# A hybrid decoder layer on eight cores: the unused output of a squaring moved to another tile, decode staging in two buffers, the decode projection in eight pieces, smaller first tables

## The reference, cut to what matters

```
def layer_inputs(h, norm_w, w_in, pos):
    hn = rms_norm(h, norm_w)
    proj = hn @ w_in
    ...
    u, gp, q, k, v, gr = jnp.split(proj, [o1, o2, o3, o4, o5], axis=-1)
    q = rotary(split_heads(q).astype(jnp.float32), pos)
    k = rotary(split_heads(k).astype(jnp.float32), pos) * (HEAD_DIM ** -0.5)
...
    # prompt group: fresh sequences, zero initial state
    u, gp, q, k, v, gr = layer_inputs(h_p, norm_w[l], w_in[l], pos_p)
    pool_o, buf_p = pool_mixer(u, buf0, pos_p, w_pool[l], pool_scale[l])
    S_p, ret_o = retention_prompt(q, k, v, log_g)
    h_p = h_p + merge_branches(pool_o, gp, ret_o, gr, ret_norm_w[l], w_out[l])
    # sample group: continue from carried state
    ...
```

## Time and profile before

| what | value |
|---|---|
| median of 3 runs (lowest to highest) | 598.63 us (596.15 to 598.93) |
| the profiled execution's own time | 599.85 us |
| span of its slowest core (core 6); all cores | 598.3 us; 589.3 to 598.3 us |
| PE / PE weight load busy | 561.6 us (94%) / 317.7 us (53%) |
| DVE / ACT / POOL busy | 389.7 / 264.7 / 110.4 us |
| DMA | 79.05 MB, 132 GB/s over the span |

### The profile page before, as it was taken

The page is one execution under the profiler, slowest core; times in us unless marked ns, Lnnn a source line. Parts: engine busy times, 40 slices in busy tenths (PEclk is TensorE's granted clock), DMA queues, the critical chain, the costliest instruction groups (busy, mean ns, idle before and its releaser), DMA issues.

```text
span 598.3 us, 13978 instructions; the slowest of 8 cores (589.3 to 598.3 us)
## 1 busy us (share of the span) xinstructions
PE 561.6 (94%) x4540; PEld 317.7 (53%) x4540; DVE 389.7 (65%) x1010; ACT 264.7 (44%) x822; POOL 110.4 (18%) x133
## 2 busy tenths in 40 slices
PE   2799998988999998999999999999999999999994
PEld 1244455674545544565564646546464646556672
DVE  3358645657865856668557676868577683954665
ACT  3245454743532632543434545454453544544332
POOL 4330001120200112111112222140322220221010
PEclk9799998997999999999999999999999999999898
DMA  8999996597444624523356764567664662627203
GB/s 166 208 172 211 168 189 146 104 119 138 89 98 103 147 89 109 160 76 90 107 143 163 160 154 134 130 191 142 181 126 138 139 161 95 143 91 153 41 3 110
DMA packets 76066, 79.05 MB, mean 132 GB/s; under 512 B 55566, under 2 KB 58270, under 8 KB 74060
## 3 DMA queue, kind: packets, MB, share of 16 engines
q1 hardware_dynamic: 71836, 56.63, 37.7%
q0 software_dynamic: 4016, 21.28, 20.7%
q10 hardware_dynamic: 144, 0.26, 0.1%
HBM read 64.86 MB, written 18.41 MB: 139 GB/s over the span
## 4 chain that ended last, share of the span: by engine, by line
PE 83%; DMA 7%; DVE 4%; issue 3%; ACT 2%; POOL 1%; SPq 0%; DVEq 0%; POOLq 0%; ACTq 0%
PE pp L592 44%; PE pp L904 18%; PE pp L609 8%; DMA w_in_bf<-w_in 2%; PE pp L845 2%; DMA pbp<-F 2%; PE pp L826 2%; DMA hnTs<-hn 2%; PE pp L967 2%; PE pp L714 1%; PE pp L755 1%; PE pp L757 1%; PE pp L731 1%; PE pp L546 1%; DMA xr<-x 1%
## 5 line engine op out<-in xcount | busy, mean ns | idle before, releaser
L592 PE MATMUL pp<-w_in_bf,hnTs 128*128 128x512 bf16 x1120 | 261.6, 385 | 1.9 <-DMA w_in_bf<-w_in 1.1
L592 PEld LDWEIGHTS pp<-w_in_bf,hnTs 128*128 128x128 bf16 x1120 | 106.0, 99 | 124.0 <-issue 14.3
L904 PE MATMUL pp<-w_out_bf,yT 128*128 128x512 bf16 (+1 forms) x464 | 100.5, 372 | 0.8 <-PE pp L904 0.2
L511 POOL TENSOR_TENSOR sm<-sm,nh 128x4 f32<-128x4 f32 (+2 forms) x49 | 44.5, 908 | 262.1 <-DVE sm L508 258.2
L630 ACT ACTIVATE F<-pp,pack 128x128 f32<-128x128 f32 (+1 forms) x208 | 59.2, 370 | 49.1 <-PE pp L592 33.9
L904 PEld LDWEIGHTS pp<-w_out_bf,yT 128*128 128x128 bf16 x464 | 44.3, 98 | 52.0 <-issue 3.4
L961 POOL TENSOR_TENSOR scr<-vM,pack 16x512 bf16<-16x512 bf16 x32 | 36.3, 1136 | 116.4 <-PE pp L967 108.1
L609 PE MATMUL pp<-hnTs,w_in_bf 128*128 128x128 bf16 x896 | 53.1, 219 | 0.0
L911 ACT ACTIVATE pp<-xr 128x512 f32<-128x512 f32 x30 | 18.0, 601 | 78.8 <-DVE xr L909 64.0
L609 PEld LDWEIGHTS pp<-hnTs,w_in_bf 128*128 128x128 bf16 x896 | 51.1, 98 | 2.1 <-issue 0.2
L793 DVE SCALAR_TENSOR_TENSOR ry<-pp,sm,G 128x128 bf16<-128x128 f32 x104 | 29.2, 343 | 19.6 <-POOL sm L511 19.5
(11 more groups left out here) (180 smaller groups left out, 723.8 us busy)
## 6 DMA issues: line engine op xcount, KB each, us to landing
w_in_bf<-w_in POOLq DMA_DIRECT2D x11, 1024.0 KB, 35.6
scr<-S_in SPq DMA_DIRECT2D x32, 256.0 KB, 3.4
Ss<-scr SPq DMA_DIRECT2D x32, 256.0 KB, 3.6
xr<-x SPq DMA_DIRECT2D x15, 512.0 KB, 4.4
y<-xr SPq DMA_DIRECT2D x15, 512.0 KB, 2.9
xA<-x SPq DMA_DIRECT2D x12, 512.0 KB, 4.0
w_out_bf<-w_out POOLq DMA_DIRECT2D x4, 1024.0 KB, 11.3
w_out_bf<-x POOLq DMA_DIRECT2D x2, 512.0 KB, 11.0
```

The source lines that it names most:

```text
L511: P.op("pool", lambda e: e.tensor_tensor(out=rs[r0:r1, c0:c0 + n], in0=rs[r0:r1, c0:c0 + n], in1=nh[r0:r1, 0:n], op=ALU.pow), reads=[rsk, ...
L592: r = e.matmul(bk(b)[:T, :], lhsT=h.ap[:, kc * T:(kc + 1) * T], rhs=w_in_bf[:, blk, kc, :], start=(kc == 0), stop=(kc == 7))
L904: r = e.matmul(bk(b)[:T, 0:w], lhsT=yap[:, kc * 128:kc * 128 + T], rhs=w_out_bf[:, kc, sl], start=(kc == 0), stop=(kc == 15))
```

## The change

A1's squares go to hnT[t] instead of `hn` for tiles from 5 on; the normalised rows still go to `hn`. The `rstd` of tile 2 gets the same false dependence that tile 0's had (it stands behind the first eviction of tile 1's transpose). Rotary scratch comes in pairs: in the first phase three (one with the PSUM bank as second scratch, two with both halves in wo12 to wo15) in place of five single ones. The two halves of tile 0's pool input are staged through F0 and `hn` in place of F0 alone. The 128 matmuls of `outp(0)` become eight tasks of 16. The first table load (`pack`) is cut from 496 to 112 columns (248 KB before, 112/496 of it now), the other 384 columns (mask and band) come on POOL's queue behind the power for tile 2, and three cosine tables move behind tile 4's x. In the scheduler the modelled POOL queue starts at 5.0, the w_out loads carry 2.0 of padding; `fill` is not used by any task.

```
-        wire = {"sp": 0.0, "pool": 0.0}
+        wire = {"sp": 0.0, "pool": 5.0}
...
-    Fsets = ([F0h[0], wof(12), wof(13), wof(14), wof(15)], [F0h[0], F0h[1]], [F0h[0]])
+    hnf = Buf(hn_t[:, :].bitcast(F32), ["hn"])
+    Fsets = ([(F0h[0], None), (wof(12), wof(13)), (wof(14), wof(15))], [(F0h[0], None), (F0h[1], None)], [(F0h[0], hnf)])
...
-        dma("pool", w_out_bf[:, b * 4:(b + 1) * 4, :].rearrange("p a b -> p (a b)"), w_out[b], [], ["wo%d%s" % (i, z) for i in range(4 * b, 4 * b + 4) for z in ("", "b")], 1 << 21, queue="w")
+        dma("pool", w_out_bf[:, b * 4:(b + 1) * 4, :].rearrange("p a b -> p (a b)"), w_out[b], [], ["wo%d%s" % (i, z) for i in range(4 * b, 4 * b + 4) for z in ("", "b")], 1 << 21, queue="w", pad=2.0)
...
-        P.op("act", lambda e: e.activation(out=hb.ap[:T, :], in_=xb.ap[:T, :], func=AF.Square,
+        junk = hb if t <= NG else hnT[t]
+        P.op("act", lambda e: e.activation(out=junk.ap[:T, :], in_=xb.ap[:T, :], func=AF.Square,
                                            accum_out=ss_x[:T, c:c + 1]), reads=xb.k + (["ss_x1"] if t == 2 else []),
-             writes=hb.k + ["ss_x%d" % c], cost=c_act(1, D, acc=1))
-        rstd(ss_x, rs_x, c, 1, 0, T, 1.0 / D, "ss_x%d" % c, "rs_x%d" % c, None, () if t else hnT[1].k[:1])
+             writes=junk.k + ["ss_x%d" % c], cost=c_act(1, D, acc=1))
+        rstd(ss_x, rs_x, c, 1, 0, T, 1.0 / D, "ss_x%d" % c, "rs_x%d" % c, None, hnT[1].k[:1] if t in (0, 2) else ())
...
-        Fa = nextF()
+        Fa, Fb = nextF()
+        fk = Fb.k if Fb else [b]
...
-                Fa = nextF()
+                Fa = (F0h[0], hnf)[hh] if t == 0 else nextF()[0]
...
-            def mmT(e, b=b):
-                r = None
-                for dc in range(8):
+            for dc in range(8):
+                def mmT(e, b=b, dc=dc):
+                    r = None
...
-            P.op("pe", mmT, reads=["yTs0", "yTs1"] + WOK, writes=[b], cost=c_pe(128, NS))
+                    return r
+                P.op("pe", mmT, reads=["yTs0", "yTs1"] + WOK + ([b] if dc else []), writes=[b], cost=c_pe(16, NS))
...
-    dma("sp", pack[:], c_pack[:, :], [], ["ident", "mask", "band", "dec", "normw", "retwc"], 1 << 18, queue="i")
+    dma("sp", pack[:, 0:112], c_pack[:, 0:112], [], ["ident", "dec", "normw", "retwc"], 1 << 16, queue="i")
...
-    load_cs(1, "w")
-    load_cs(0, "w")
     load_x(3, stage[3], "w")
     for i, t in enumerate(order0):
         if t == 0:
             load_w(WORD[1], None, ["rs_x1"])
-            load_cs(2, "w", ["rs_x2"])
+            dma("pool", pack[:, 112:496], c_pack[:, 112:496], ["rs_x2"], ["mask", "band"], 1 << 18, queue="w")
         if t == 3:
             load_x(4, stage[4], "w", ["rs_x0"])
+            for c in (1, 0, 2):
+                load_cs(c, "w")
             load_w(WORD[2])
```

More of the change, by code:

```diff
@@ L54, in ps, with op @@
         return self.stack.enter_context(self.nc.psum_tensor(name, list(shape), dt))
-    def op(self, eng, fn, reads=(), writes=(), sem=None, cost=0.2, size=0, bias=0.0, queue=None, pad=0.0):
+    def op(self, eng, fn, reads=(), writes=(), sem=None, cost=0.2, size=0, bias=0.0, queue=None, pad=0.0, fill=None):
         t = Task(eng, fn, reads, writes, sem, cost, size, bias)
-        t.pad = pad
+        t.pad, t.fill = pad, fill
         if queue is not None:
@@ L152, in bank_at @@
             return best
-        while len(done) < len(tasks):
+        total, real = len([t for t in tasks if t.fill is None]), 0
+        while real < total:
             pick = None
@@ L168, in schedule @@
                         s = max(s, ba[0])
-                    cand.append((s, t))
+                    if t.fill is None or s < t.fill:
+                        cand.append((s, t))
                 if not cand:
@@ L172, in schedule @@
                 lo = min(c[0] for c in cand)
+                work = [c for c in cand if c[1].fill is None]
+                if work and min(c[0] for c in work) <= lo + 0.1:
+                    cand = work
                 s, t = max((c for c in cand if c[0] <= lo + SLACK[e]), key=lambda c: (c[1].rank, -c[1].i))
@@ L193, in schedule @@
             done.add(t)
+            real += t.fill is None
             order.append(t)
@@ L570, in ev @@
             return r
-        P.op("dve", ev, reads=[b, "normw"], writes=d.k[:1] if n < 8 else d.k, cost=c_dve(n, T))
+        P.op("dve", ev, reads=[b, "normw"], writes=d.k[:1] + ["go"] if n < 8 else d.k, cost=c_dve(n, T))
         if n < 8:
@@ L622, in rotary, with fb @@
         b = pj_mm(t, (2 if which == "q" else 3) * D + hh * 512)
-        Fa = nextF()
+        Fa, Fb = nextF()
+        fk = Fb.k if Fb else [b]
+        def fb():
+            return Fb.ap if Fb else bk(b)
         dslot = (0 if t else 2) if which == "q" else (1 if t else 3)
@@ L641, in rot @@
         def rot(e):
-            f1 = bk(b)[:T, :].rearrange("p (h two j) -> p h two j", h=4, two=2)
+            f1 = fb()[:T, :].rearrange("p (h two j) -> p h two j", h=4, two=2)
             e.scalar_tensor_tensor(out=f1[:, :, 0, :], in0=f0[:, :, 1, :], scalar=-1.0, in1=sinb,
@@ L645, in rot @@
             return e.tensor_tensor(out=f1[:, :, 1, :], in0=f0[:, :, 0, :], in1=sinb, op=ALU.mult)
-        P.op("dve", rot, reads=Fa.k + cs.k, writes=[b], cost=c_dve(2, 256))
+        P.op("dve", rot, reads=Fa.k + cs.k, writes=fk, cost=c_dve(2, 256))
         P.op("dve", lambda e: e.tensor_tensor(out=f0, in0=f0, in1=cosb, op=ALU.mult),
-             reads=Fa.k + [b] + cs.k, writes=Fa.k, cost=c_dve(1, 512))
-        P.op("dve", lambda e: e.tensor_tensor(out=dst, in0=Fa.ap[:T, :], in1=bk(b)[:T, :], op=ALU.add),
-             reads=Fa.k + [b], writes=dk, cost=c_dve(1, 512))
+             reads=Fa.k + fk + cs.k, writes=Fa.k, cost=c_dve(1, 512))
+        P.op("dve", lambda e: e.tensor_tensor(out=dst, in0=Fa.ap[:T, :], in1=fb()[:T, :], op=ALU.add),
+             reads=Fa.k + fk, writes=dk, cost=c_dve(1, 512))
     def p_u(t):
@@ L873, in mmT @@
                                      rhs=yTs[:, kc * NS:(kc + 1) * NS], start=(kc == 0), stop=(kc == 15))
-                return r
-            P.op("pe", mmT, reads=["yTs0", "yTs1"] + WOK, writes=[b], cost=c_pe(128, NS))
+                    return r
+                P.op("pe", mmT, reads=["yTs0", "yTs1"] + WOK + ([b] if dc else []), writes=[b], cost=c_pe(16, NS))
             r1, r2 = sc67.ap[:, 0:128], sc67.ap[:, 128:256]
```

## The result

The changed kernel takes 607.46 us (median), the kernel before 598.78 us beside it: 1.0145 of before, with a 95% interval of 1.0098 to 1.0192. It is slower by 1 to 2%, where 595.5 us was forecast, and it lies above the range of 587 to 602.5. The profiled execution took 607.68 us; its slowest core is now core 3.

The account below looks back on a forecast made before the run. PE's own work bounds the kernel, so only windows where PE idles or runs at slow clock can be gained. +2.3 - 3.3 + 0.7 - 2.8 = -3.1 off 598.63 gives 595.5 us, range 587 to 602.5.

Parts of the forecast that it names:

- Squares into hnT, tile 5: Before tile 5's first projection: a new stall plus slow clock, 8.3 us, in place of the 6 removed; +2.3.
- I take 6.6: PE's stall for tile 5's transpose behind two w_out loads, bounds 0 and 7.6 us, taken near the upper one.
- the overlap: At tile 5's transpose: 1 us allowed off the 7.6 us stall of waiting for both w_out loads.
- The 6 us taken away there: At 133 to 143 us: PE's 4.0 us wait and 1.7 of slow clock go, with some shorter matmuls; -6.
- Rival 1: Tile 5's transpose shares with the loads (587.2 us) or waits for one only (589.6); chance 0.3 for both.
- rival 2: DVE waits for w_out block 2 and holds PE up; up to 601.5 us, 603.5 with the start; chance 0.12.
- 76 to 104 us: PE's waits and slow clock in these windows shrink through the changed order; ceiling 5.0, floor 0, two thirds taken: -3.3.
- Start: First tiles: POOL's added issues make tile 3's power later, at 21.4 against 20.57 us; +0.7 (0 to +2).
- that hides it: At the start: PE's wait at 24.73 for tile 3's transposed rows hides a first projection late at 15 to 16.
- The POOL term: At the start: eleven issues of 0.57 us behind tile 0's power put tile 3's power at 21.4; not hidden, +0.7.
- State steps: PE's operand waits at state steps (2.0 and 1.0 us) get covered by other work; -2.8 (0 to -3.0).
- Decode projection: The 128 matmuls in pieces may fill PE's 1.4 us idle in 556 to 591; 0, bounds -1.4 and +1.

Follow-up runs that it names:

- e3: Changed kernel in its own order, but the loads of w_out blocks 2 and 3 both wait for tile 5's transpose to land; 607.17 us, 1.0074 of before.
- e8: Kernel before, with only the squares of tiles 6 to 16 moved to hnT; 600.24 us, 0.9983 of before.
- e10: Changed kernel without its first edit, the squares of all tiles in hn as before; 592.55 us, 0.9905 of before.
- e2: Changed kernel in its own order, but the load of w_out block 3 waits for tile 5's transpose to land; 599.33 us, 0.9956 of before.
- e5: Kernel of e1 with the squares of tile 16 in hn as well; 593.76 us, 0.9863 of before.
- e9: Kernel before, with the squares of all tiles from 5 on moved to hnT, tile 5 included; 600.99 us, 1.0024 of before.
- e1: Changed kernel with the squares of tile 5 alone back in hn; 594.5 us, 0.9862 of before.

## Why the prediction was wrong

The mechanism of the largest term was right and its size was not, and the gain set against it was not that edit's in this order. The other misses are terms that the sum did not have or took as hidden. By its own steps:

- **Squares into hnT, tile 5 (+2.3 predicted, about +7 measured).** The step that failed is "I take 6.6": the stall was 11.3 us. PE's other work behind tile 2's gate took 14.4 us (14.5 predicted). In that time the transpose was put at landing 21.1 us after the gate, with the overlap, and landed at 25.6. The square began 0.7 us late, behind an eviction, and took the loads and the transpose with it (3.8, 6.4 and 7.2 us after the square). The first load took 13.0 us and not 11.4, the second landed 7.1 us after it and not 5.7, and the 1 us allowed for an overlap was not there. The sum had no term for what SP's queue moves beside the loads: in 139 to 146 us it was x's load, 104 packets and 0.43 MB against 103 and 0.84 of POOL's queue. In e3, with x's loads nearly through before it, the first load took 9.9 us. That fits the longer loads, but no run takes x's load alone away.
- **The 6 us taken away there.** e8 bears the mechanism out (the wait for kdM falls to 0.8 us on every core). But e10 has no hole at 133 without this edit, so the rest of the change removes it too, and the edit paid nothing back: with 1.9 us of slow clock its stall cost 13.2 us. The sum below still counts the hole as gone, whichever edit did it: 13.2 - 6 = 7.2.
- **Rival 1 (chance 0.3).** Its times, 587 to 590, did not come, and a transpose that waits for one load only is ruled out: e3, e2 and the changed kernel give 3.1, 11.4 and 17.7 us. Its row for sharing was misread: kT's transpose was issued at 119.44, 1.1 us ahead of the load, and landed at 123.8, when the load's first packets moved. The upper end of the range, 602.5, is neither of rival 2's two times, 601.5 and 603.5.
- **The same edit at the other tiles (not in the sum).** The prediction costed the new wait, for the last projection that reads the slot, at tile 5 only. At tile 16 it moves the normalise from 486 us (before) to 506, into a stretch where DVE is the one waited for: 3.2 us idle in 505 to 526, and eight matmuls in 3.31 us in place of 1.89. e5 takes the waits away there, without a gain in time that could be measured.

```profile
512.94 3.31 PE L600 MATMUL pp<-w_in_bf,hnTs 128*128 128x512 bf16 x8 [1.67 <-DVE qd L661]
```

- **76 to 104 us (-3.3 predicted).** -5.0, the ceiling: PE is busy throughout both windows. The cause is not the first edit: in e10, without it, PE is busy in all of 76 to 104, in e8, with it alone, in 24.5 of the 28 us. Which of the other edits it is was not tried.
- **Start (+0.7 predicted, 0 to +2).** The first projection of tile 3 stood at 24.73 on core 6, now on core 3 at 27.68, +2.9. Core against itself it is +0.2 (core 7) to +4.0 (core 3), so the 2.9 is rough. The tokens arrived at 10.9 (10.6 predicted). The step that failed is "that hides it": the first projection, now at 16.60 in place of 13.83, passes its lateness on, because on ACT tile 3's square stands behind its eviction (before too: 17.89 and 18.64). The POOL term did not bind, for POOL idled 2.56 us ahead of tile 3's power.

```profile
21.58 0.60 ACT L625 ACTIVATE w_out_bf<-pp 128x512 bf16<-128x512 f32 x1 [7.66 <-PE pp L600]
22.07 1.05 ACT L535 ACTIVATE W<-w_out_bf 128x1024 bf16<-128x1024 f32 x1
```

- **State steps (-2.8 predicted).** 0.5 us of the 3.0 are left, in 270 to 290: -2.5.
- **Decode projection (0 predicted, -1.4 to +1).** The pieces let the scheduler pull the decode pooling forward in front of its load: 1.9 us of wait in 548 to 551, a term that the sum did not have.

Measured terms: +7.2, +4.6 (505 to 526), -5.0, +2.9, -2.5 and +1.9 make +9.1; the spans differ by 7.6 (605.9 - 598.3, of different cores), the medians by 8.7. That the two come near each other is in part luck: the start is taken across cores, and the 4.6 were not seen in the time when e5 took them away. The forecast's place for a wrong sign, rival 2, was not what happened in the changed kernel: DVE did stand 6.0 us for w_out, but PE was stalled by then anyway. It happened in e3.

## What to carry to other kernels

An unused output still needs a place, and the place brings its own wait: where it was moved, one has to ask at every tile who reads the new place last, and what that delays. Before a small transfer is timed, count the large loads that stand ahead of it on any queue; one load more made it 6 to 8 us later here (3.1, 11.4, 17.7), and letting it be issued ahead of both was worth 2 to 3%. When a scheduler reorders all engines, cost an edit alone on the old order and the rest of the edits without it. Here the first edit alone gave +0.2% (e9) and the rest -1.0% (e10), but both together +0.9 to 1.5%.

## What the runs showed of the hardware

A DMA transpose on SP's queue lands shortly after the last large load issued before it on POOL's queue: it took 3.1 us with none, 11.4 with one (landing 1.6 us after it) and 17.7 with two (0.9 after the second); in e9, with other transfers of SP's queue ahead of it, it landed 2.9 us after its load. A plain load on SP's queue is held too: xr, issued between the two loads, took 12.9 us and landed 0.2 us after the first, and 3.8 us with none. By the Trainium skill ("DMA: Bandwidth & Descriptors", section "Queues, rings and completion order") an engine switches between rows after each packet. The trace of the changed kernel agrees: 75 packets of POOL's queue stand against 74 of SP's in 149 to 153 us, with 0.61 and 0.02 MB, and e1 has 75 against 73 there. So the transpose does get its turns, and rival 1's sharing was wrong in what a turn is worth; from 154 us on, with the load nearly through, SP's queue moves 923 packets in 2.9 us. Two things stay open. No run changes the packet size, and in the kernel before and in e9 SP's queue moves no packet at all in 124 to 129 and 131 to 134 us, beside a load already under way, though its transfers had been issued.

Work put into a wait keeps the granted clock at 1.00 and the next matmuls at full speed (3.61 in place of 5.48 us for sixteen). The part of a slow spell that falls into the wait itself cost nothing: the clock was 0.72 in the stall of the changed kernel, and only the 1.9 us behind it were lost.
